# MoBA queries and keys computed in transposed form, with native fp32 pair scores, in one decoder layer

## What is computed

```python
def rope(x, pos):
    ...
    x1 = x[..., :half]
    x2 = x[..., half:]
    return jnp.concatenate([x1 * cos - x2 * sin, x2 * cos + x1 * sin], axis=-1)
...
        proj = u @ w_in[l]
        c_q = proj[..., :s1]
        c_kv = proj[..., s1:s2]
        k_r = proj[..., s2:s3]
        moba_qkv = proj[..., s3:].reshape(B, S, 3, MOBA_HEADS, MOBA_HEAD_DIM)
        ...
        mla_o = mla_attention(c_q, c_kv, k_r, mla_q_norm_g[l], w_mla_q_up[l],
                              mla_kv_norm_g[l], w_mla_kv_up[l], pos)
        moba_o = moba_attention(rope(moba_qkv[0], pos), rope(moba_qkv[1], pos), moba_qkv[2])
        mix = jnp.concatenate([...], axis=-1)
        h = h + rms_norm(mix @ w_out[l], attn_post_g[l])
        u = rms_norm(h, mlp_pre_g[l])
        a = jnp.square(jax.nn.relu(u @ w_up[l]))
        h = h + rms_norm(a @ w_down[l], mlp_post_g[l])
```

## Time and profile before

| | |
|---|---|
| median of 3 runs | 565.72 us (565.59 to 566.14) |
| profiled execution, its own time | 565.26 us |
| its span, first to last instruction | 563.5 us |
| mean granted PE clock over the span | 0.996 |
| PE busy | 551.0 us, 98% of the span |
| DVE, ACT, POOL busy | 70%, 53%, 17% |

### The profile page before, as it was taken

The page is one execution under the profiler, slowest core; times in us unless marked ns, Lnnn a source line. Parts: engine busy times, 40 slices in busy tenths (PEclk is TensorE's granted clock), DMA queues, the critical chain, the costliest instruction groups (busy, mean ns, idle before and its releaser), DMA issues.

```text
span 563.5 us, 7954 instructions
## 1 busy us (share of the span) xinstructions
PE 551.0 (98%) x2790; PEld 457.9 (81%) x2790; DVE 392.4 (70%) x751; ACT 297.2 (53%) x623; POOL 95.2 (17%) x156
## 2 busy tenths in 40 slices
PE   9999999999999999999999999999999999999994
PEld 8988898876766788988888888887888888888883
DVE  5349662687884366367766775569868889787897
ACT  6563261788885354454335334435454656556461
POOL 1253200355777002200000000000000001000003
PEclk9999999999999999999999999999999999999998
DMA  8931522000003750177767788678984555606403
GB/s 294 367 94 57 187 74 76 0 2 2 1 2 113 271 177 1 67 296 269 265 228 274 277 272 288 225 277 284 358 310 164 212 192 182 223 8 217 150 0 149
DMA packets 41774, 97.23 MB, mean 173 GB/s; under 512 B 2192, under 2 KB 20368, under 8 KB 38416
## 3 DMA queue, kind: packets, MB, share of 16 engines
q1 hardware_dynamic: 41312, 96.11, 48.8%
q10 hardware_dynamic: 432, 0.74, 0.4%
HBM read 81.11 MB, written 15.73 MB: 172 GB/s over the span
## 4 chain that ended last, share of the span: by engine, by line
PE 70%; DMA 18%; DVE 4%; ACT 3%; issue 2%; SPq 2%; POOL 1%; POOLq 0%; DVEq 0%; ACTq 0%
PE bank L1347 20%; PE bank L1348 19%; PE bank L1349 19%; DMA pair_sums<-stage 16%; PE bank L1371 3%; PE bank L1571 2%; PE bank L1550 2%; DMA w_raw<-in_w_up 1%; PE bank L1512 1%; ACT probs L666 1%; ACT w_hi L574 1%; DVE bank L1014 1%; DVE w_lo L897 1%; SPq L393 1%; PE bank L1400 1%
## 5 line engine op out<-in xcount | busy, mean ns | idle before, releaser
L1347 PE MATMUL bank<-uT_hi,w_hi 128*128 128x512 f32 (+1 forms) x280 | 104.2, 372 | 0.2 <-DVE w_lo L897 0.2
L1348 PE MATMUL bank<-uT_lo,w_hi 128*128 128x512 f32 (+1 forms) x280 | 103.9, 371 | 0.0
L1349 PE MATMUL bank<-uT_hi,w_lo 128*128 128x512 f32 (+1 forms) x280 | 103.8, 371 | 0.0
L1347 PE MATMUL bank<-w_hi,a_hi 128*128 128x512 f32 x224 | 87.2, 389 | 0.0
L1349 PE MATMUL bank<-w_hi,a_lo 128*128 128x512 f32 x224 | 87.2, 389 | 0.0
L1348 PE MATMUL bank<-w_lo,a_hi 128*128 128x512 f32 x224 | 87.1, 389 | 0.0
L897 DVE SCALAR_TENSOR_TENSOR w_lo<-w_raw,g_up,w_hi 128x256 fp32r<-128x256 f32 x128 | 52.0, 479 | 49.4 <-ACT w_hi L574 49.4
L574 ACT ACTIVATE w_hi<-w_raw,g_up 128x256 fp32r<-128x256 f32 x128 | 52.8, 496 | 46.5 <-DMA w_raw<-in_w_up 27.5
L574 ACT ACTIVATE w_hi<-w_raw 128x1024 fp32r<-128x1024 f32 (+2 forms) x49 | 46.8, 1001 | 51.1 <-PE bank L1349 47.3
L894 DVE TENSOR_TENSOR w_lo<-w_raw,w_hi 128x1024 fp32r<-128x1024 f32 (+1 forms) x41 | 48.9, 1234 | 19.8 <-ACT w_hi L574 19.7
L1347 PEld LDWEIGHTS bank<-uT_hi,w_hi 128*128 128x128 f32 x280 | 52.7, 188 | 9.7 <-issue 0.6
(11 more groups left out here) (165 smaller groups left out, 965.2 us busy)
## 6 DMA issues: line engine op xcount, KB each, us to landing
stage<-in_w_down SPq DMA_DIRECT2D x17, 1024.0 KB, 5.0
w_raw<-in_w_up SPq DMA_DIRECT2D x16, 1024.0 KB, 8.3
pair_sums<-stage SPq DMA_DIRECT2D x13, 1024.0 KB, 10.1
w_raw<-in_w_down SPq DMA_DIRECT2D x10, 1024.0 KB, 6.3
w_raw<-pair_sums SPq DMA_DIRECT2D x10, 1024.0 KB, 4.8
w_raw<-in_w_in SPq DMA_DIRECT2D x6, 1024.0 KB, 7.1
w_raw<-in_w_out SPq DMA_DIRECT2D x4, 1024.0 KB, 4.9
stage<-pair_sums SPq DMA_DIRECT2D x3, 1024.0 KB, 4.7
```

Of the source, the lines that this page charges most:

```text
L1347: nc.tensor.matmul(out, lh, rh, start=start, stop=False)
L1348: nc.tensor.matmul(out, lh, rl, start=False, stop=False)
L1349: return nc.tensor.matmul(out, ll, rh, start=False, stop=stop)
```

## The change

The MoBA queries and keys come out of the projection already transposed. `half_group` uses the weight as the stationary operand and the tokens as the moving one, in as many matmuls of the same size; bank `4 + j` then holds 128 rows of projected columns by 512 tokens. The columns of `w_in` are reordered on their way in (`half_columns`), so that banks 4 and 5 hold the first and second 32-wide halves of four heads, banks 6 and 7 those of the other four. A rotation is then one product of a bank with the cosines, one of its partner bank with the sines (both full banks, DVE) and a subtraction or an addition on POOL. The row norm, now along the columns, is spread by four PE transposes into bank 7, copied by DVE (`r_cols`) and multiplied into the tables (`turn`). The 32-row halves are joined to 64-row heads in `mqT` and `mkT` by 32 DMA transfers of 32 rows by 512 (`half_tiles`, on SP). The pair scores take `mqT` and `mkT` as native fp32 operands, one matmul per head and token tile. The pairs' `q_prep`, `k_prep`, `q_part` and `k_part` are gone, the third slots of `qT` and `kT` too, and `out_piece`, `p_part` and the first out tiles move.

```diff
-        mq_nat = sb("mq_nat", [P, NT, HW], stack=att)
-        mk_nat = sb("mk_nat", [P, NT, HW], stack=att)
+        mqT = sb("mqT", [P, HEADS // 2, S], stack=att)
+        mkT = sb("mkT", [P, HEADS // 2, S], stack=att)
...
         def ACT_COPIES(i, n):
-            return n == 0 or n == 2 and (i < HEADS or i % 2 == 0 or i in (HEADS - 1, HEADS + 1))
+            return n == 0 or n == 2 and (i < HEADS - 2 or i % 2 == 1 and i < NH - 1)
...
-        OUT_PIECES = {6: [0]}
-        PAIR_PIECES = {4: [1], 5: [2], 6: [3, 4], 7: [5, 6], 8: [7]}
+        PAIR_PIECES = {4: [0], 5: [1], 6: [2, 3], 7: [], 8: [4, 5, 6, 7]}
...
+            def half_tiles(which):
+                for j in range(NT):
+                    g, s = j // 2, j % 2
+                    sp.wait_ge(roped, NT * which + j + 1)
+                    for h in range(HEADS // 2):
+                        r0 = MOBA_D * (h % 2) + 32 * s
+                        sp.dma_start((mqT, mkT)[which][r0:r0 + 32, 2 * g + h // 2, :],
+                                     rt1[32 * h:32 * h + 32, j, :]).then_inc((mq_in, mk_in)[which][j], 16)
...
-            for i in range(3, 6):
+            in_chunk(3)
+            sp.dma_start(turn[:, :, :], rope_cols).then_inc(turn_in, 16)
+            for i in range(4, 6):
                 in_chunk(i)
             sp.dma_start(g_up[:, :], mlp_pre_g).then_inc(g_up_in, 16)
             chunk(Q_CH, w_q_v, 2 * HEADS * QH)
+            half_tiles(0)
             chunk(KV_CH, w_mla_kv_up.rearrange("o p n -> p o n"), HEADS * P)
             in_chunk(6)
             in_chunk(7)
+            half_tiles(1)
...
-                nc.gpsimd.tensor_tensor((mq_nat, mk_nat)[n // NT][:, t, :], rt1[:, n % 2, :], rt2[:, n % 2, :],
-                                        ALU.add).then_inc(roped, 1)
+                nc.gpsimd.tensor_tensor(rt1[:, j, :], rt1[:, j, :], rt2[:, n % 2, :],
+                                        ALU.add if j % 2 else ALU.subtract).then_inc(roped, 1)
...
             in_lo(2)
+            dve.wait_ge(r_full, 1)
+            nc.vector.tensor_copy(r_cols[:, :], ps[7][:, :]).then_inc(r_ready, 1)
             in_lo(3)
+            dve.wait_ge(turn_in, 16)
+            dve.wait_ge(r_ready, 1)
+            for s in range(2):
+                last = nc.vector.tensor_tensor(turn[:, s, :], turn[:, s, :], r_cols[:, :], ALU.mult)
+            step(last)
...
-                dve.wait_ge(proj, NT * group + t + 1)
+                dve.wait_ge(proj, NT * group + (j | 1) + 1)
+                if n >= NT:
+                    dve.wait_ge(mq_in[j], 64)
                 if n >= 2:
                     dve.wait_ge(roped, n - 1)
...
+                nc.vector.tensor_tensor(rt1[:, j, :], ps[4 + j][:, :], turn[:, 0, :], ALU.mult)
+                nc.vector.tensor_tensor(rt2[:, n % 2, :], ps[4 + (j ^ 1)][:, :], turn[:, 1, :],
+                                        ALU.mult).then_inc(rope_m, 1)
...
                 pair_maxes(m, [6, 7])
+                p_part(a, 2)
                 o_part(m - 2)
                 pair_sums(m, 2)
...
+            def half_group(g, before_tile):
+
+                for part in range(2):
+                    r = IN_CH[2 * g + part]
+                    for j in range(NT):
+                        before_tile(part, j)
+                        if j == 0:
+                            pe.wait_ge(w_ready, r + 1)
+                        for k in range(4):
+                            w = slice(HW * k + P * j, HW * k + P * j + P)
+                            last = mm3(ps[4 + j][:, :], w_hi[w_slot(r)][:, w], w_lo[w_slot(r)][:, w],
+                                       uT_hi[:, 4 * part + k, :], uT_lo[:, 4 * part + k, :],
+                                       part == 0 and k == 0, part == 1 and k == 3)
...
+            def before_queries(part, j):
+
+                if part == 0 and j == 2:
+                    pe.wait_ge(rstd, NT)
+                    for t in range(NT):
+                        last = nc.tensor.transpose(ps[7][:, P * t:P * t + P], stat[:, 0, t, 3:4].to_broadcast([P, P]),
+                                                   ident[:, :])
+                    last.then_inc(r_full, 1)
+                if part == 0 and j == 3:
+                    pe.wait_ge(r_ready, 1)
+
+            def before_keys(part, j):
+
+                if part == 0:
+                    pe.wait_ge(rope_m, (j | 1) + 1)
...
-                    for n, (q, k) in enumerate(((qT_hi, kT_hi), (qT_hi, kT_lo), (qT_lo, kT_hi))):
-                        for h in range(2):
-                            b, c = PAIR_AT[t][h]
-                            r = slice(MOBA_D * h, MOBA_D * h + MOBA_D)
-                            last = nc.tensor.matmul(ps[b][:, c:c + w], q[s][r, tok], k[s][r, 0:w], start=n == 0, stop=n == 2)
-                            if n == 2 and t != 2:
-                                last.then_inc(s_full, 1)
+                    for h in range(2):
+                        b, c = PAIR_AT[t][h]
+                        r = slice(MOBA_D * h, MOBA_D * h + MOBA_D)
+                        last = nc.tensor.matmul(ps[b][:, c:c + w], mqT[r, m - FIRST, tok], mkT[r, m - FIRST, 0:w],
+                                                start=True, stop=True)
+                        if t != 2:
+                            last.then_inc(s_full, 1)
...
+            for arrived in mq_in + mk_in:
+                pe.wait_ge(arrived, 64)
             probs_T(0, PT_ORDER)
...
                 probs_T(a, PT_ORDER[3:])
                 probs_T(b, PT_ORDER[:3])
-                if m < FIRST + 2:
-                    k_prep(2 * m + 4)
-                    q_prep(2 * m + 4)
-                else:
-                    probs_T(b, PT_ORDER[3:])
+                probs_T(b, PT_ORDER[3:])
+            out_ready(0)
+            out_tile(0, 0)
+            probs_T(NH - 2, PT_ORDER)
             weighted(NP - 2, range(NT))
-            probs_T(NH - 2, PT_ORDER)
-            out_early(0)
```

More of the change, by code:

```diff
@@ L205, in build @@
         kT_full, kh, kl = sem("kT_full"), sem("kh"), sem("kl")
+        mq_in, mk_in = [[sem(f"{n}{j}_in") for j in range(NT)] for n in ("mq", "mk")]
+        turn_in, r_full, r_ready = sem("turn_in"), sem("r_full"), sem("r_ready")
         s_full, s_nb, s_exp = sem("s_full"), sem("s_nb"), sem("s_exp")
@@ L996, in _ @@
             dve.wait_ge(roped, 2 * NT)
+            for j in range(2):
+                dve.wait_ge(mk_in[j], 64)
             for t in range(NT):
@@ L1132, in _ @@
             p_part(NH - 1, 2)
+            dve.wait_ge(wo_ready, 1)
+            for n in PAIR_PIECES[NP]:
+                out_piece(n)
             o_part(NP - 1)
@@ L1405, in _ @@
             pe.wait_ge(consts, 2)
-            group(1, lambda part, t: None)
+            half_group(1, before_queries)
             pe.wait_ge(cn_ready, 2 * NT)
@@ L1416, in _ @@
             last.then_inc(krT_full, 1)
-            group(2, lambda part, t: part == 0 and pe.wait_ge(rope_m, t + 1))
+            half_group(2, before_keys)
             pe.wait_ge(w_ready, Q_CH + 1)
@@ L1627, in _ @@
                 probs_T(b, PT_ORDER[:3])
-                if m < FIRST + 2:
-                    k_prep(2 * m + 4)
-                    q_prep(2 * m + 4)
-                else:
-                    probs_T(b, PT_ORDER[3:])
+                probs_T(b, PT_ORDER[3:])
+            out_ready(0)
+            out_tile(0, 0)
+            probs_T(NH - 2, PT_ORDER)
             weighted(NP - 2, range(NT))
-            probs_T(NH - 2, PT_ORDER)
-            out_early(0)
             probs_T(NH - 1, PT_ORDER)
-            out_early(1)
+            for t, b in SPARE:
+                for kk in range(2):
+                    out_rows(t, b, 0, kk)
             weighted(NP - 1, range(NT))
-            for c in range(2):
-                for t in range(1, NT):
-                    if c == 0 and t == NT - 1:
-                        pe.wait_ge(ol, NH // 2)
-                    last = out_tile(t, c)
-                last.then_inc(w_used, 1)
+            for t in range(1, NT):
+                for b in range(2):
+                    if (t, b) not in SPARE:
+                        for kk in range(2):
+                            if t == NT - 1:
+                                pe.wait_ge(ol, NH // 2)
+                            last = out_rows(t, b, 0, kk)
+            last.then_inc(w_used, 1)
+            out_ready(1)
+            for t in range(NT):
+                last = out_tile(t, 1)
+            last.then_inc(w_used, 1)
             pe.wait_ge(wo_ready, NO)
@@ L1733, in _, with rope_constants, half_columns @@
                     last.then_inc(d_used, 1)
[L1736 removed]
+def rope_constants(seq, width, repeat):
     import numpy as np
[L1740 to L1746 removed]
+    half = width // 2
+    inv = (np.float32(1.0) / np.float32(10000.0) ** (np.arange(half, dtype=np.float32) / np.float32(half))).astype(np.float32)
+    ang = (np.arange(seq, dtype=np.float32)[:, None] * inv[None, :]).astype(np.float32)
```

(11 more changed lines are left out.)

182 lines of the change are left out of this document (52 added, 130 removed).

## The result

The changed kernel takes 562.11 us (median of 4 runs, 561.74 to 562.46) against 565.74 of the kernel before in the same session: a ratio of 0.9933, 95% interval 0.9921 to 0.9945, so 3.6 us faster. Its profiled execution took 562.25, that of before 565.26; the two traces differ by 3.0 us.

What follows compares the result with a forecast made beforehand. PE, busy 98% of the span, was taken to bound the kernel. Terms 0.44 + 0 + 0.3 − 2.4 − 3.1 = −4.8 gave 560.5 us profiled, 561.0 median; own range 559.5 to 562.5, over cases 558.0 to 565.0.

Steps and rivals of the forecast that it cites:

- rival (b): In the pair steps, a native product costs as much as four fp32r products, 3.0 per pair: 562.2 us, chance 0.18.
- 1, front: Before the MLA heads: four added row-norm transposes cost PE 0.44 us, added DVE work stays hidden: +0.44 us.
- bound of 0.7: In front: possible loss in us, counted as 0, if one more DVE copy delays the rotations PE's group 2 needs.
- 2, joins: DMA transfers joining query and key halves, 16 per half, issued in 5.9 to 9.4 us, cost 0.
- my upper end: Longest time forecast for SP to issue 16 join transfers: 9.4 us, at 0.59 each.
- 3, eight waits: Semaphore waits ahead of PE's first probabilities, already met, still cost issue time: +0.3 us, within 0 to 0.5.
- 4, end of the heads: End of the MLA heads: removed transposes 1.32, their wait 0.32, shorter wait for exponentials 0.76: −2.4 us.
- the last wait: First pair scores' wait of 0.93 us for ACT's exponentials of head 7, forecast to shrink by 0.76.
- 5, pair steps: Four pair steps: 7.2 plus three of 7.8, 30.6 us against 33.66, with transposes gone from PE: −3.1 us.
- The cycle: In pair steps, a loop from PE through DVE and POOL back to PE, 7.8 us, sets three of four.
- rival (a): In pair steps, the loop through DVE and POOL does not bind, steps take 7.2: 559.2 us, chance 0.18.
- Rival (c): Pair scores of two heads do not run beside each other in the array, 4.6 per pair: 568.2 us, chance 0.11.

Runs made afterwards that it cites:

- Run 5: The changed kernel once more, unedited: 562.08 us, ratio 0.9936.
- Run 6: The changed kernel with the products of the tables reading the row norm from PSUM bank 7, ahead of a weight split, without the copy: 561.78 us.
- Run 8: The changed kernel with DVE's remainder of the first output part ahead of a maximum in the last MLA heads: 562.62 us.
- run 7: The changed kernel with DVE's reciprocals of head a ahead of the remainder of the output part in each pair step: 561.70 us.
- run 4: The changed kernel with the same scores reordered, all tiles of one head before those of the other: 565.51 us.
- run 3: The changed kernel, native scores kept, but ACT and DVE still make the pairs' hi and lo parts, which PE awaits and nothing reads: 567.58 us.
- run 2: The changed kernel with its scores back in three fp32r products, ACT and DVE making hi and lo parts from the joined tiles: 566.75 us.

## Why the prediction was right

The forecast was 561.0, the time is 562.1, inside its own range of 559.5 to 562.5. It is nearer than its terms. They were summed for the profiled execution, to −4.8, and the trace shows −3.0; 0.6 of the 1.7 between them is made up by chance, because the median lies 0.14 below the profiled execution now and lay 0.46 above it before. And 562.1 is as good as rival (b)'s number, 562.2; only the terms tell the two apart. Step by step:

**1, front (+0.44).** Mis-sized. The four transposes cost what they should, but the sentence "I expect it to lie under DVE's waits for POOL's norms" failed: the products of the tables, put there, held POOL up, so the cover itself grew longer. Run 5 shows +1.59 up to group 2, most of it a wait for DVE's rotations (0.86 by the profile, 1.1 from start to start) that had been kept as a bound of 0.7. Run 6 takes 0.5 of it back by making the products earlier, with one operand from PSUM.

**2, joins (0).** Right in time, wrong in one figure. SP's queue of the changed kernel:

```profile
48.68 10.13 SPq L355 DMA_DIRECT2D mqT<-rt  x16
58.85 0.58 SPq L342 DMA_DIRECT2D w_raw<-in_w_mla_kv_up  x1
```

Sixteen transfers take 10.1 us to issue, 0.63 each, more than my upper end, and the load behind them is 2.1 us late. Nothing waits for it: group 2 to the first probabilities is 61.34 us against 61.35.

**3, eight waits (+0.3).** Nothing: the same 61.34.

**4, end of the heads (−2.4).** −1.77. I let 0.17 of the last wait stand, 0.57 stands, so it gave 0.36 and not 0.76; and 0.51 appeared that `k_prep` had covered, 0.44 of it new. From start to start the three sets of transposes with their wait were worth 1.85, not 1.64. The first pair's scores begin at 139.50, not near 138. Run 8 shows that this is no slack of PE's: the chain through DVE, ACT and POOL paces the heads.

**5, pair steps (−3.1).** −2.72. The cycle was forecast at 7.8 and is 7.78; PE's own work was forecast at 7.2 and is 7.59, because native scores take 2.56 a pair, not 2.36, and the twelve transposes 1.70, not 1.53, as the last two wait 0.23 for DVE's copy of the bank (on PE's weight loads). So rival (a) was not to be had: under the cycle there are only 0.19 us (run 7). Rival (b)'s 3.0 is not reached. The Trainium skill's four passes ("FP8 and Floating Point Precision", TensorE Precision Notes), counted against three products, spoke against the change; the trace does not show passes (each native matmul has two records), but the score tiles cost 13% more than in three fp32r products, not a third. Rival (c) did not happen; run 4 shows that its mechanism exists when the heads don't alternate.

What the prediction had wrong was where the gain comes from. "So the scores bring nothing. What PE sheds here are five sets of four transposes" is half of it. The halves of the change, each by its trace (front as the shift of the first probabilities against before, heads from there to the first pair scores, then the four steps):

| | front | heads | pair steps | median |
|---|---|---|---|---|
| before | 0 | 31.38 | 33.66 | 565.7 |
| native scores alone (1) | +0.3 | 30.61 | 34.00 | 564.4 |
| transposed alone (2) | +1.0 | 31.48 | 33.60 | 566.8 |
| both | +1.5 | 29.61 | 30.94 | 562.1 |

Neither half, as built here, shortens the pair steps. With native scores alone PE keeps the transposes and dearer scores; with transposed computing alone ACT and DVE keep the parts, and those set the pace (run 3). Only both together take 2.7 us off, and pay for the front that the transposed form costs. How much of the 2.7 the reordering gives to native scores stays open: the waits for ACT's copies that it ends were 2.2 us before and 1.3 with native scores alone. The prediction's sum for the step came out near because it priced the step with both bounds lowered, and ascribed the result to one.

## What to carry to other kernels

Where the paths through two engines are nearly as long as each other, price each half of a change against the other engine's floor: freeing PE alone bought nothing here, freeing ACT and DVE alone 1.3 us, both, with the reordering, 3.6. A wait that looks like cover for added work is only that if the engine waited for does not share something with the one that gets the work. And the shortest idle in front of PE is not a gain to be had until the chain behind it has been followed: run 8 removed 0.51 us of waiting, and the heads took 0.2 longer.

## What the runs showed that I had not expected

A POOL operation of 0.19 us took 1.78 beside DVE products with both operands in SBUF, and its usual time when one came from PSUM. Native fp32 scores of two heads in the two halves of the array take 1.93 us when the heads alternate and 2.88 when they don't. The start of group 1 lies between 23.2 and 24.3 us from run to run, and it does not set the time: with starts of 24.31, 23.54, 23.31 and 23.16 (first profile, runs 5, 7 and 8) group 2 begins at 48.55, 48.66, 48.77 and 48.70, as PE waits there for DVE's rotations. And one idle of 2.44 us on PE was followed by 4.6 us at a lower granted clock in run 3, and by none in run 2.
